# A state-space core: two heads' value products side by side, and decay differences made by TensorE under a mask in PSUM

## The reference, cut to what matters

```
a_cum = cumsum(dt * a)                             # [T] per head and direction
seg   = a_cum[t] - a_cum[s]                        # kept where s <= t (backward: s >= t)
lmat  = exp(where(mask, seg, -inf))                # decay
y[t]  = sum_s (C[t] . B[s]) * lmat[t, s] * dt[s] * x[s]      # [T, 64]
out   = y_forward + y_backward + d_skip * x
```

## Time and profile before

| | |
|---|---|
| median of 3 runs | 4190.03 us (4185.27 to 4192.93) |
| the profiled execution, its own time | 4193.89 us |
| its span in the trace | 4192.0 us |
| PE, DVE, ACT, POOL busy, share of the span | 91%, 48%, 37%, 10% |
| mean granted TensorE clock | 0.948 |
| the core block in the trace | 157.67 to 262.09 us |

### The profile page before, as it was taken

The page is one execution under the profiler, slowest core; times in us unless marked ns, Lnnn a source line. Parts: engine busy times, 40 slices in busy tenths (PEclk is TensorE's granted clock), DMA queues, the critical chain, the costliest instruction groups (busy, mean ns, idle before and its releaser), DMA issues. The chain is left out here.

```text
span 4192.0 us, 52129 instructions
## 1 busy us (share of the span) xinstructions
PE 3800.1 (91%) x20592; PEld 2946.4 (70%) x20592; DVE 2012.7 (48%) x3106; ACT 1530.7 (37%) x2399; POOL 400.1 (10%) x356
## 2 busy tenths in 40 slices
PE   7898889789999898898889999989988789999988
PEld 5456777678778786675667878876676567877876
DVE  4879555664433325446365443333536546443332
ACT  4454333433332324325353232233324444332232
POOL 0036340000011012100000001100010000001100
PEclk9899999889999998899999999999999999999999
DMA  3011002113322232020212322222111112332222
GB/s 108 16 53 46 2 3 88 34 37 116 96 90 94 79 93 66 31 72 9 103 42 90 92 87 95 95 78 78 51 58 34 76 46 81 96 95 86 95 80 71
DMA packets 83487, 289.31 MB, mean 69 GB/s; under 512 B 9168, under 2 KB 9296, under 8 KB 82000
## 3 DMA queue, kind: packets, MB, share of 16 engines
q1 hardware_dynamic: 83136, 286.30, 21.5%
q10 hardware_dynamic: 144, 0.15, 0.0%
HBM read 284.32 MB, written 2.10 MB: 68 GB/s over the span
## 5 line engine op out<-in xcount | busy, mean ns | idle before, releaser
L547 DVE TENSOR_TENSOR weights_lo_r<-raw_weights,weights_hi_r 128x1024 fp32r<-128x1024 f32 (+2 forms) x554 | 634.8, 1146 | 1726.1 <-ACT weights_hi_r L541 1725.9
L541 ACT ACTIVATE weights_hi_r<-raw_weights 128x1024 fp32r<-128x1024 f32 (+2 forms) x554 | 547.6, 989 | 1829.3 <-PE ps L614 1794.4
L613 PE MATMUL ps<-xn_r,weights_hi_r 128*128 128x512 f32 x2816 | 1116.0, 396 | 0.0
L612 PE MATMUL ps<-xn_hi,weights_hi_r 128*128 128x512 f32 x1952 | 804.7, 412 | 77.8 <-DVE xn_r L607 26.7
L614 PE MATMUL ps<-xn_hi,weights_lo_r 128*128 128x512 f32 x1952 | 777.7, 398 | 0.0
L613 PEld LDWEIGHTS ps<-xn_r,weights_hi_r 128*128 128x128 f32 x2816 | 539.6, 192 | 126.2 <-issue 10.3
L612 PEld LDWEIGHTS ps<-xn_hi,weights_hi_r 128*128 128x128 f32 x1952 | 377.1, 193 | 193.9 <-issue 81.4
L614 PEld LDWEIGHTS ps<-xn_hi,weights_lo_r 128*128 128x128 f32 x1952 | 377.4, 193 | 82.9
L614 PE MATMUL ps<-y_r,weights_lo_r 128*128 128x512 f32 x1056 | 419.6, 397 | 0.0
L612 PE MATMUL ps<-y_r,weights_hi_r 128*128 128x512 f32 x1056 | 418.0, 396 | 1.2 <-PEq L858 1.2
L612 PE MATMUL ps<-hidden_hi,weights_hi_r 128*128 128x512 f32 x528 | 216.6, 410 | 31.9 <-DVE hidden_r L607 31.9
(11 more groups left out here) (508 smaller groups left out, 5283.7 us busy)
## 6 DMA issues: line engine op xcount, KB each, us to landing
raw_weights<-in_w_ffn_dram SPq DMA_DIRECT2D x132, 512.0 KB, 3.7
raw_weights<-in_w_down_dram SPq DMA_DIRECT2D x48, 512.0 KB, 3.5
raw_weights<-in_w_out_dram SPq DMA_DIRECT2D x24, 512.0 KB, 3.8
bias_table<-in_window_bias_dram SPq DMA_DIRECT2D x8, 1280.0 KB, 10.3
raw_weights<-in_w_down_dram SPq DMA_DIRECT2D x24, 384.0 KB, 3.1
raw_weights<-in_w_hgrn_dram SPq DMA_DIRECT2D x16, 512.0 KB, 3.5
raw_weights<-in_w_mix_ssm_dram SPq DMA_DIRECT2D x16, 512.0 KB, 3.8
raw_weights<-in_w_a_qk_dram SPq DMA_DIRECT2D x16, 512.0 KB, 3.5
```

The costliest lines, as they stand in the source:

```text
L541: act.activation(self.k.w_hi[:, g % 2, 0:chunk.width], self.k.raw[:, slot, 0:chunk.width], ACT.Copy)\
L547: dve.tensor_tensor(self.k.w_lo[:, g % 2, 0:chunk.width], self.k.raw[:, slot, 0:chunk.width], self.k.w_hi[:, g % 2, 0:chunk.width].bitcast ...
L612: pe.matmul(out, w_hi, x_hi, start=start, stop=False)
L613: pe.matmul(out, w_hi, x_lo, start=False, stop=False)
```

## The change

It has three parts.

1. **Order and value products.** The steps are taken in pairs: for heads 2m and 2m + 1, key tile 0 of both, then tile 1 of both, and so on (`place`). `weigh(q)` on PE issues the four value products of a pair together, with the output halves in turn: forward of the even head, forward of the odd head, backward of the even, backward of the odd. Products go to banks 6 and 7.
2. **Differences by PE.** `spread_head` goes. `subtract(n)` makes only what step n needs: for each direction one matmul that copies the running sums of head h for the needed columns (weights of 32 rows: the high parts on partitions 0 to 15, the low parts on 16 to 31, so that one matmul adds both), and one matmul with the 128x128 identity as weights and 128 columns of a mask, 0 or -1e30, added to the own tile. So four matmuls per step, in fp32r, into a ring of three pairs of banks. The low parts are moved to partitions 16 to 31 by a transfer that SP issues in the setup block; DVE makes the mask and the picking matrix there.
3. **Exponentials from PSUM.** ACT reads PSUM, adds the column of the key's sum as bias and takes the exponential in one instruction per direction, two per step, into a ring of six slots. DVE multiplies in place. All bounding passes and `prob` go.

The diff, cut to its core:

```diff
-        decay = sb("decay", [P, 3, T + P])
-        prob = sb("prob", [P, 2, T + P])
+        decay = sb("decay", [P, 5, T + P])
+        last_decay = k.x[:, 5:7, :].rearrange("p a t -> p (a t)")[:, 0:T + P]
...
-        ident_r = spare[0:H, 4, 0:H]
+        both_parts, below = spare[0:2 * H, 0:2, :], spare[:, 4, 0:2 * P].rearrange("p (r t) -> p r t", r=2)
+        ident_r, pick = spare[:, 7, 0:P], spare[0:2 * H, 7, P:P + H]
...
-                act.activation(ident_r, k.const("ident", H)[:, 0:H], ACT.Copy).then_inc(ident_copied, 1)
+                act.activation(ident_r, k.const("ident"), ACT.Copy).then_inc(ident_copied, 1)
...
-                act.activation(colpos[:, :, :, :], small[:, :, 0:2, :], ACT.Copy).then_inc(cols_ready, 1)
+
+            @block.sync
+            def _(sp):
+                sp.wait_ge(acum_split, 2)
+                sp.dma_start(spare[H:2 * H, 0:2, :].bitcast(F32), acum_lo.bitcast(F32)).then_inc(lo_in, 16)
+                sp.wait_ge(lo_in, 16)
...
+                dve.tensor_tensor(pick, k.const("ident", 2 * H)[:, 0:H], k.const("ident", 2 * H)[:, H:2 * H], ALU.add)\
+                    .then_inc(pick_ready, 1)
+                for r, kept in enumerate(("le", "ge")):
+                    dve.tensor_scalar(below[:, r, :], k.const(kept), -1.0, 1.0e30, ALU.add, ALU.mult)\
+                        .then_inc(below_ready, 1)
...
+            RING = 6
+            PAIRS = H // 2 * NT
+
+            def place(n):
+
+                m, j = divmod(n // 2, NT)
+                return 2 * m + n % 2, j
+
+            def slot(n):
+                return decay[:, n % RING, :] if n % RING < RING - 1 else last_decay
+
+            def differences(n, r):
+
+                j = place(n)[1]
+                return k.ps[:, 2 * (n % 3) + r, 0:(j + 1) * P if r else T - j * P]
+                def subtract(n):
+                    h, j = place(n)
+                    if n >= 3:
+                        pe.wait_ge(decayed, 2 * (n - 2))
+                        ts, own = (slice(0, (j + 1) * P), j * P) if r else (slice(j * P, T), 0)
+                        out = differences(n, r)
+                        pe.matmul(out, pick[:, h:h + 1].broadcast_to([2 * H, P]), both_parts[:, r, ts], start=True,
+                                  stop=False)
+                        mm = pe.matmul(out[:, own:own + P], ident_r, below[:, r, :], start=False, stop=True)
+                def weigh(q):
+                    m, j = divmod(q, NT)
+                    pe.wait_ge(prob_ready, 2 * q + 2)
+                    if j == 0 and m >= 2:
+                        pe.wait_ge(y_ready, m - 1)
+                    for r in range(2):
+                        for half in range(2):
+                            h, o = 2 * m + half, k.ps[64 * half:64 * half + 64, 6 + m % 2, :]
+                            ts, part = (slice(0, (j + 1) * P), slice(T - j * P, T + P)) if r else \
+                                (slice(j * P, T), slice(0, T - j * P))
+                            mm = pe.matmul(o[:, ts], xdt[r][:, j, h * SSM_P:(h + 1) * SSM_P], slot(2 * q + half)[:, part],
+                                           start=(j == 0 and r == 0), stop=(j == NT - 1 and r == 1))
+                    mm.then_inc(pair_used, 1)
+
+                for q in range(PAIRS + 2):
+                    if q < PAIRS:
+                        subtract(2 * q)
+                        subtract(2 * q + 1)
+                    if q >= 2:
+                        weigh(q - 2)
+                for n in range(2 * PAIRS):
+                    h, j = place(n)
+                    act.wait_ge(spread, n + 1)
+                    if n >= RING:
+                        act.wait_ge(pair_used, (n - RING) // 2 + 1)
+                    for r, part in enumerate((slice(0, T - j * P), slice(T - j * P, T + P))):
+                        act.activation(slot(n)[:, part], differences(n, r), ACT.Exp, bias=colneg[:, j, r, h:h + 1])\
+                            .then_inc(decayed, 1)
+                    dve.wait_ge(pair_used, NT * (m + 1))
+                                             in1=bank(k.ps, 6 + m % 2), op0=ALU.mult, op1=ALU.add)\
+                for n in range(2 * PAIRS):
+                    h, j = place(n)
+                    dve.wait_ge(decayed, 2 * n + 2)
+                    dve.tensor_tensor(slot(n), slot(n), cbm[:, h // 8, j, :], ALU.mult).then_inc(prob_ready, 1)
+                    if n >= 2 * NT and n % (2 * NT) == 6:
```

More of the change, by code:

```diff
@@ L1377, in ssm_branch @@
         colneg = sb("acum_cols", [P, NT, 2, H])
-        colpos = sb("acum_cols_pos", [P, NT, 2, H])
         coldt = sb("dt_cols", [P, NT, 2, H])
@@ L1389, in ssm_branch @@
         project(k, [("w_dt", dt_raw, 1.0), ("w_xbc", raw[:, :, PAD:PAD + T], 1.0)], k.xn, norm,
-                beside=SsmConvolution(raw, act_x, prob[:, :, 0:T], dt_raw, dt, acum, a_exp))
+                beside=SsmConvolution(raw, act_x, decay[:, 3:5, 0:T], dt_raw, dt, acum, a_exp))
         with ExitStack() as inner:
             (acum_split, ident_copied, cols_turned, cols_ready, dt_cols_ready, x_turned, x_used, cb_done,
-             cb_used) = semaphores(k, inner, "acum_split ident_copied cols_turned cols_ready dt_cols_ready "
-                                   "x_turned x_used cb_done cb_used")
+             cb_used, lo_in, pick_ready, below_ready) = semaphores(
+                k, inner, "acum_split ident_copied cols_turned cols_ready dt_cols_ready "
+                "x_turned x_used cb_done cb_used lo_in pick_ready below_ready")
             block = inner.enter_context(nc.Block())
@@ L1462, in ssm_branch @@
         with ExitStack() as inner:
-            spread, bounded, own_bounded, decayed, prob_ready, tile_used, y_ready = semaphores(
-                k, inner, "spread bounded own_bounded decayed prob_ready tile_used y_ready")
-            OWN = NT // 2
+            spread, decayed, prob_ready, pair_used, y_ready = semaphores(
+                k, inner, "spread decayed prob_ready pair_used y_ready")
+            RING = 6
+            PAIRS = H // 2 * NT
             block = inner.enter_context(nc.Block())
+            def place(n):
+                m, j = divmod(n // 2, NT)
+                return 2 * m + n % 2, j
@@ L1474, in spread_head @@
                     for r in range(2):
-                        out, row = bank(k.ps, 4 + 2 * (h % 2) + r), ident_r[:, h:h + 1].broadcast_to([H, P])
-                        pe.matmul(out, row, acum_hi[:, r, :], start=True, stop=False)
-                        mm = pe.matmul(out, row, acum_lo[:, r, :], start=False, stop=True)
-                    mm.then_inc(spread, 1)
[L1481 to L1496, removed]
@@ L1550, in _ @@
                         output(n // (2 * NT) - 1)
-                weigh(NT * H - 1)
                 output(H // 2 - 1)
```

27 lines of the change are left out of this document (removed).

## The result

The changed kernel takes **4287.41 us** (median of four runs, 4280.32 to 4290.23) against 4191.48 us for the kernel before (four runs, 4185.27 to 4193.14): 95.9 us more, ratio 1.0229, 95% interval 1.0211 to 1.0247. The forecast was 4288, by 98 us more.

The account below looks back on a forecast made before the run. PE was taken as the bound, by a factor of two over ACT and DVE, at 1.2 GHz: 6.23 us a pair, stage 200.2 against 104.4 us (+96), next stage +2. That +98 gave a median of 4288, range 4200 to 4300.

Parts of the forecast that it names:

- clock in the block: TensorE's clock in the changed stage: stays at 1.2 GHz (0.50) throughout, chance 0.52.
- eight difference matmuls of a pair, 1.2 GHz: PE's differences per pair: eight shape changes 2.40, picked rows 1.07, mask 0.43 us.
- value products of a pair, 1.2 GHz: PE's value products per pair: 2.13 us plus 0.20 for their change of shape.
- two closing rounds, products alone: End of the changed stage: two rounds of products without differences, at the low clock, 4.5 us.
- case B: Rival: the clock rises in the changed stage and stays, 3.58 us a pair, stage 121.1 us, kernel 4207; chance 0.18.
- start of the next stage: The stage behind, at clock 1.00 before the change, would begin at a low clock: about +2 us.
- The shape change: Each of a pair's eight difference matmuls pays for changing array shape: 0.20 us at the high clock, 0.30 at 1.2 GHz.
- Case D: Rival: shape changes cost PE only 0.10 us at the high clock, 2.78 us a pair, kernel 4181; chance 0.09.
- C: Rival: the clock alternates in the changed stage, half at each level, +57 us, kernel 4247; chance 0.15.
- ACT, DVE and the setup: ACT at most 1.86, DVE at most 1.83 us a pair, both below PE; setup edits cost 0, 0.9 without cover.
- The halves: Value products of two heads run at the same time in column halves: PE saves 1.1 us per pair.
- case E: Rival: the halves don't run at the same time, +2.13 us a pair, +166 in all, kernel 4356; chance 0.03.

Follow-up runs that it names:

- e9: Changed kernel with picking matmuls padded to 64 rows, ten full matmuls ahead of the loop and three more in each of its first two rounds: 4218.06 us.
- e10: Changed kernel, picking matmuls kept at 32 rows, with ten full matmuls ahead of the loop and three more in each of its first two rounds: 4271.76 us.
- e2: Changed kernel with each step's two picking matmuls first and its two mask matmuls behind them, so fewer shape changes: 4254.54 us.
- e1: Changed kernel with picking matmuls padded with zeros to 128 rows, the shape of the mask matmuls: 4166.72 us, ratio 0.9951 to the kernel before.
- e3: Changed kernel with one more matmul per pair (128 rows, 512 columns, result overwritten): 4272.43 us, from runs of 4261.90 and 4282.96.
- e6: e1 with both heads' products in columns 0 to 63, sharing one half of the array, and two full matmuls ahead of the loop: 4198.41 us.
- e8: Changed kernel with picking matmuls padded to 64 rows, nothing added ahead of the loop: 4288.76 us.
- e5: e1 with all value products of a pair's first head issued ahead of those of the second: 4167.82 us.
- e7: Changed kernel with picking matmuls padded to 64 rows and ten full matmuls ahead of the loop: 4292.46 us.

## Why the prediction was right

The time (4288 against 4287.4) is not right by luck of a sum; its terms can be read one by one. One of them, the clock, was a judgement between levels at 0.52 and not a derivation: no row had 32-row and 128-row matmuls in turn.

| term of the forecast | forecast | measured |
|---|---|---|
| clock in the block | 0.50 throughout | 0.50 from 157.5 to 352 |
| eight difference matmuls of a pair, 1.2 GHz | 2.40 + 1.07 + 0.43 = 3.90 us | 3.86 (251.93 to 255.79) |
| value products of a pair, 1.2 GHz | 2.13 + 0.20 = 2.33 us | 2.34 (6.20 - 3.86) |
| a pair | 6.23 us | 6.20 |
| two closing rounds, products alone | 4.5 us | 3.2 (350.93 to 354.15) |
| the block | 200.2 us | 197.5 |
| a pair at 2.4 GHz (case B) | 3.58 us | 3.61 (e9, e10) |
| start of the next stage | +2 us | 0 (see below) |
| whole kernel | +98 us | +95.9 |

**The shape change.** The price came from a place where whole groups change shape and from rows of the attention at the low clock, and it held between single instructions: 0.29 to 0.30 us at 1.2 GHz, 0.21 at 2.4 GHz. e2 confirmed it by taking out four changes of a pair, e1 by making the differences one shape; not all of the 0.3 goes with a change (0.23 in e2). Case D, which needed 0.14 or less, did not occur. By the Trainium skill, "TensorEngine Tiling (Array Packing)", section "Key Properties", a change of tiling mode drains the engine; it gives no price. The trace fits, with 0.29 to 0.30 us at each change, but shows only that time and not what the engine does in it.

**The clock.** Chances were spread over three clocks, and the likeliest came: eight gapless 16-row records with the clock at 0.50 behind them were a better guide than the absence of gaps. By the Trainium skill, "TensorE: Matmul & The Clock Gate", section "Why this matters for your kernels", a TensorE kept busy has its full clock; PE was busy for 189.00 of 189.00 us at 0.50, so the measurement disagrees for this work. What the prediction had not seen is how near the other cases lay: e3 shows the clock going up and down with 128-row work added (C), e9 one that stays (B). e9 with its added matmuls took 4218 us; case B, without them, was forecast at 4207.

**ACT, DVE and the setup** were costed at nothing, since PE covers them, and that held. ACT waited 120.8 + 9.9 us for PE. In the setup block three operations of DVE and the low halves' DMA are new:

```profile
136.00 0.34 DVE L1445 TENSOR_SCALAR x_r<-consts 128x128 fp32r<-128x128 f32 x2
136.02 0.61 SPq L1435 DMA_DIRECT2D x_r<-x_r  x1
137.60 0.29 DVE L1451 TENSOR_TENSOR cb_masked<-ps,consts 128x128 f32<-128x128 f32 x1 [1.26 <-PE ps L1413]
```

The operation behind them began at 137.60, before it was 137.74; the gap of 1.62 us is 1.26 now. The page gives 2.3 us for the 64 KB of the low halves, from issue to landing, so they lay there long before 157.47. The block began at 157.47, where it was 157.67.

**The halves** run at once also with fp32, 128 rows and 512 columns, so case E is out, and e6 gives the gain: 1.07 us a pair, forecast 1.1.

**The one step that failed** is the clock at the block's end, which was taken to be low. The last two rounds have products alone, and the clock rose to 1.00 before 353 us. So the closing rounds took 3.2 us and not 4.5, and the next stage began at the full clock: from the block's end to that stage's first SCALAR_TENSOR_TENSOR on DVE (L1602, before L1601) it took 13.8 us (354.96 to 368.77), as before (262.09 to 275.86), where +2 was forecast. No row stood behind the "3 to 4 us" of a low stretch in that term.

With the experiments, the pair's 3.10 us become 6.20 in three steps: all parts of the change with one shape, 2.45 (e1), so -0.65; the shape changes at 2.4 GHz, 3.61 (e9), so +1.16; the low clock, 6.20, so +2.59. Over 32 pairs that is -21, +37 and +83 us, +99 in all, against +93.1 measured for the block, whose first and last rounds are shorter. The change would have paid, and paid in e1, had its picking matmuls used all rows. The idea was good and a detail of its layout cost it 120 us.

**Still open** is by what the clock is granted. e8 beside e9 says that what went before matters, e9 beside e10 that the rows in use may, e3 that 128-row work can go with a rise for a time; each of e8, e9 and e10 is a single execution, and only repeats would settle it. No run tells why added rows that hold only zeros bring the full clock (e1), or why e10's clock held for 44 us.

## What to carry to other kernels

Matmuls that follow each other closely should have one shape in the array. Padding a thin one with zero rows costs nothing in columns. Here each shape change that went spared 0.17 us at 2.4 GHz (1.16 us for the seven among a pair's differences, e1 beside e9) and 0.23 at 1.2 GHz (e2), and the clock rose to 2.4 GHz and stayed. Before moving work to a TensorE that "has time", price it at both clocks and read the granted clock of a stretch with the same shapes: 100% busy at 0.50 is half an engine. And when a change combines parts, one that loses 96 us may hold one that gains 32 (e6 beside e1).

## What was not expected of the hardware

- TensorE started a later matmul for the free half of the columns 14 ns behind the first one (e5), though another matmul of the first half stood between them. The program's order of the halves made no difference (4167.82 and 4166.72 us, blocks 83.0 and 82.8).
- More work was not more time: with 32 added matmuls of 128 rows the block was 9 us shorter in one execution (e3, 188.3 against 197.5), through the clock, and the kernel's other execution was no slower than the changed kernel.
- What stood in front of the loop went with a different clock far into it: the same full rounds ran at 0.50 in e8 (158.4 to 355 us) and at 1.00 in e9 (to 285 us and beyond), one execution each. With 32 rows it was lost after 44 us of gapless work (e10), and with 64 rows within the two rounds that had no products (e7).
- With one shape, a 128-column mask matmul held PE for 0.06 us, but a picking matmul of 384 columns ahead of it held it for 0.22, and for 0.28 as the first of a round, where the columns are 0.16 (e1). The prediction's column prices give 0.74 us for a pair's eight difference matmuls, and e1 has 1.17 (200.28 to 201.45, with the change to the products' shape at its end): short matmuls cost more than their columns even with one shape. Each has weights of its own, but no run shows that these are the reason.
